# Triangular inversions of the recurrence: their first four levels on 32x32 tiles of TensorE's array in place of 64x64

## The reference

```python
lmat = jnp.where(strict, jnp.einsum("nbhcd,nbhsd->nbhcs", k_beta, kc) * decay, 0.0)
eye = jnp.eye(C, dtype=q.dtype)
rhs = jnp.concatenate([v_beta, k_beta * jnp.exp(gc)[..., None]], axis=-1)
sol = lax.linalg.triangular_solve(eye + lmat, rhs, left_side=True, lower=True, unit_diagonal=True)
```

## Time and profile before

| | us |
|---|---|
| median of 3 runs | 3714.71 |
| lowest, highest run | 3710.28, 3719.96 |
| the profiled execution, its own time | 3723.04 |
| span of the profiled instructions | 3721.2 |
| TensorE busy in the span | 3501.6 |
| VectorE busy in the span | 2381.4 |
| ScalarE busy in the span | 1693.0 |

### The profile page before, as it was taken

One profiled execution on the slowest core, in us unless ns is written; L12 is line 12 of the kernel. 1 busy time (PEld: TensorE's weight loads), 2 busy tenths in 40 slices (PEclk: granted clock), 3 DMA queues, 4 the chain that ended last, 5 costly groups with the idle time before them and its releaser, 6 DMA issues. The chain is left out here.

```text
span 3721.2 us, 74594 instructions
## 1 busy us (share of the span) xinstructions
PE 3501.6 (94%) x28666; PEld 2970.6 (80%) x28666; DVE 2381.4 (64%) x4144; ACT 1693.0 (45%) x2572; POOL 109.8 (3%) x159
## 2 busy tenths in 40 slices
PE   9999998997999999999899998888788899999998
PEld 8998887787888888888788965766676788888887
DVE  5758885665688888656643553676665766666555
ACT  5546773323455555444312443444443455555333
POOL 0000000000000000000000000221110000000000
PEclk9999999898999999999999998999997999999999
DMA  5547665444445555555322464000002455555553
GB/s 199 180 143 277 256 254 187 147 159 158 169 158 180 180 181 182 194 193 182 128 90 102 149 226 168 6 7 8 6 6 83 157 187 186 190 180 181 185 186 135
DMA packets 83114, 572.03 MB, mean 154 GB/s; under 512 B 9585, under 2 KB 11889, under 8 KB 18129
## 3 DMA queue, kind: packets, MB, share of 16 engines
q1 hardware_dynamic: 81216, 560.60, 42.5%
q0 software_dynamic: 1680, 8.36, 0.6%
HBM read 566.82 MB, written 2.10 MB: 153 GB/s over the span
## 5 line engine op out<-in xcount | busy, mean ns | idle before, releaser
L252 DVE TENSOR_TENSOR w_lo<-raw,w_hi 128x1024 fp32r<-128x1024 f32 x880 | 1037.2, 1199 | 270.7 <-ACT w_hi L245 261.4
L245 ACT ACTIVATE w_hi<-raw 128x1024 fp32r<-128x1024 f32 (+1 forms) x877 | 894.1, 1038 | 640.9 <-PE po L287 308.1
L286 PE MATMUL po<-hh,w_hi 128*128 128x512 f32 x2816 | 1000.2, 400 | 21.2 <-DVE hh L391 9.2
L287 PE MATMUL po<-hh,w_lo 128*128 128x256 f32 x2816 | 789.8, 280 | 0.0
L286 PEld LDWEIGHTS po<-hh,w_hi 128*128 128x128 f32 x2816 | 530.3, 188 | 164.3 <-issue 18.7
L287 PEld LDWEIGHTS po<-hh,w_lo 128*128 128x128 f32 x2816 | 533.1, 189 | 0.0
L286 PE MATMUL po<-ff,w_hi 128*128 128x512 f32 x1408 | 494.7, 396 | 7.9 <-DVE ff L1831 7.9
L287 PE MATMUL po<-ff,w_lo 128*128 128x256 f32 x1408 | 395.1, 281 | 0.0
L286 PEld LDWEIGHTS po<-ff,w_hi 128*128 128x128 f32 x1408 | 265.6, 189 | 69.8 <-issue 8.5
L287 PEld LDWEIGHTS po<-ff,w_lo 128*128 128x128 f32 x1408 | 267.4, 190 | 0.0
L266 PE MATMUL po<-hh,w_lo 128*128 128x256 f32 x928 | 266.0, 287 | 0.6 <-DVE w_lo L252 0.6
(11 more groups left out here) (577 smaller groups left out, 6416.7 us busy)
## 6 DMA issues: line engine op xcount, KB each, us to landing
raw<-ffn_up SPq DMA_DIRECT2D x176, 1024.0 KB, 4.8
raw<-w_in SPq DMA_DIRECT2D x112, 1024.0 KB, 4.9
raw<-ada SPq DMA_DIRECT2D x86, 1024.0 KB, 6.0
raw<-ffn_down SPq DMA_DIRECT2D x64, 1024.0 KB, 5.0
raw<-w_out SPq DMA_DIRECT2D x32, 1024.0 KB, 4.8
raw<-ffn_down SPq DMA_DIRECT2D x32, 768.0 KB, 4.2
raw<-glu SPq DMA_DIRECT2D x16, 1024.0 KB, 6.6
ada_third<-ada SPq DMA_DIRECT2D x10, 1024.0 KB, 6.5
```

What stands on the lines that cost most here:

```text
L245: act.activation(w_hi[:, k % 4, 0:width], raw[:, k // 2 % ring, (k % 2) * PW:(k % 2) * PW + width], ACT.Copy).then_inc(hi_ready, 1)
L252: dve.tensor_tensor(w_lo[:, k % 4, 0:width], raw[:, k // 2 % ring, (k % 2) * PW:(k % 2) * PW + width], w_hi[:, k % 4, 0:width].bitcast(F32 ...
L286: pe.matmul(halves(bank), hi, pair[:, :, t, :], start=first and n == 0, stop=False)
L287: mm = pe.matmul(po[bank][:, 0:T], lo, pair[:, 0, t, :], start=False, stop=last and n == len(tiles) - 1)
```

## The change

A new helper `quads_pe` issues a group of levels 1 to 4 as matmuls of 32x32 by 32x32. Partition group g (32 rows) uses the tile at row group g and column group g of the array, so four tiles on the array's diagonal. In the mask product each tile computes its own diagonal block of the 64x64 result (`own`: its columns start at 0 or 32); in the sum product it computes the 32 packed columns once. The order is block m, direction e, tile g. A group now has 32 matmuls, which will be 64 matmuls and 64 weight loads in a trace. The parts of the result outside the diagonal blocks aren't written any more; VectorE still reads all 64 columns after the mask product and multiplies them by a mask that is zero there. Level 5 uses `blocks_pe` as before. Nothing changes on VectorE, ScalarE or in the waits.

```diff
--- before.py
+++ after.py
@@ -1115,17 +1115,39 @@
             for e in range(2):
                 mm[e].then_inc(sets[e][0], 1)
 
+        def quads_pe(pe, sets, outs, lhs, rhs, own):
+
+            settle(pe)
+            for m in range(4):
+                mm = []
+                for e in range(2):
+                    for g in range(4):
+                        r, h = slice(32 * g, 32 * g + 32), g % 2 * 32
+                        c = h if own else 0
+                        last = pe.matmul(outs[e][r, m * C + c:m * C + c + 32], lhs[e][r, m, h:h + 32],
+                                         rhs[e][r, m, c:c + 32], start=True, stop=True)
+                    mm.append(last)
+            for e in range(2):
+                mm[e].then_inc(sets[e][0], 1)
+
         def inv_mask_pe(pe, n, sets, l):
             for by_pe, by_dve, (i_a, i_t, i_tt, i_p), b, want in sets:
                 pe.wait_ge(by_dve, n * 17 + (3 * l if l == 1 else 3 * l - 1))
-            blocks_pe(pe, n, sets, 2 * l - 1, [s[3][0] for s in sets], [s[2][0] for s in sets], [s[2][1] for s in sets])
+            outs, lhs, rhs = [s[3][0] for s in sets], [s[2][0] for s in sets], [s[2][1] for s in sets]
+            if l < 5:
+                quads_pe(pe, sets, outs, lhs, rhs, True)
+            else:
+                blocks_pe(pe, n, sets, 2 * l - 1, outs, lhs, rhs)
 
         def inv_sum_pe(pe, n, sets, l):
             for by_pe, by_dve, (i_a, i_t, i_tt, i_p), b, want in sets:
                 pe.wait_ge(by_dve, n * 17 + (3 * l + 1))
             lhs = [i_p if l == 5 and want == "tt" else i_tt for _, _, (i_a, i_t, i_tt, i_p), b, want in sets]
             rhs = [i_tt if l == 5 and want == "tt" else i_p[:, :, 0:C // 2] for _, _, (i_a, i_t, i_tt, i_p), b, want in sets]
-            blocks_pe(pe, n, sets, 2 * l, [s[3][1] for s in sets], lhs, rhs)
+            if l < 5:
+                quads_pe(pe, sets, [s[3][1] for s in sets], lhs, rhs, False)
+            else:
+                blocks_pe(pe, n, sets, 2 * l, [s[3][1] for s in sets], lhs, rhs)
 
         def inv_first_dve(dve, n, sets):
             for by_pe, by_dve, (i_a, i_t, i_tt, i_p), b, want in sets:
```

## The result

The changed kernel takes 3765.32 us (median of 4 runs, 3761.88 to 3770.2) against 3712.93 us before: the ratio is 1.0135, with a 95% interval of 1.0115 to 1.0154. It is slower by 52 us, outside the range of the prediction.

What follows compares the result with a forecast made beforehand. The recurrence, chiefly the inversion's products on TensorE, was taken to bound the kernel. Array gain -13.5 us plus late instructions +16 us gave +2.5 us, forecast 3717 us against the median 3714.71, range 3690 to 3755.

Steps and rivals of the forecast that it cites:

- What bounds the kernel: Only the 495 us recurrence decides; the inversion's products (line 1114) hold 19.8% of its chain of waits, 98 us.
- Array time: In groups of levels 1 to 4, the array needs 0.51 us instead of 0.93, a gain of 0.42.
- The pace of the instructions: In the new groups, matmuls start between 0.008 and 0.0145 us apart, so a group takes 0.51 to 0.93 us.
- waiting groups: Inversion groups that begin after a pause, 64 of 128 changed; forecast to stay at 0.93 us, together +1.3 us.
- queued groups: Inversion groups standing behind other matmuls, 64 of 128 changed; forecast at 0.51 us, together -21.8 us of TensorE time.
- Changes of tile size: Beside the new groups, each switch costs 0.09 us; 0.11 charged per queued group, 0.05 per waiting group.
- 0.66 us of the end: Weight of each microsecond in the inversion groups: the chain counts 98 of 149 us, turning -20.5 into -13.5 us.
- rival 4: Recurrence: shorter bursts idle TensorE, half the 128 groups run at the lower clock; 3777 us, chance 0.04.
- Delivery of the instructions: Recurrence: doubled instructions arrive late in 119 packets, 28 more stalls at 0.87 us each; +16 us.
- Rival 2: Recurrence: TensorE starves, two packets in three stall, 71 more stalls; +27 us, 3742 us, chance 0.21.
- Rival 3: New groups: tiles don't run side by side when writing one bank; +17 to +104 us, chance 0.08 including the floor on starts.
- the floor on starts: New groups: matmuls start no closer than 0.025 us, a group takes 1.6 us; +66 us, 3781 us, chance 0.03.

Runs made afterwards that it cites:

- e5: The changed kernel with 32 matmuls of 128 columns in each group of levels 1 to 4, most products using another block's matrix; ratio 1.0000 to the kernel before.
- e2: The changed kernel with half the weight loads, each matmul over two blocks' columns (64), blocks 2 and 3 using another block's matrix; ratio 1.0016 to the kernel before.
- e3: The changed kernel with 64 columns in each matmul of levels 1 to 4, same instructions and tiles; 3761.6 us, ratio 1.0132 to the kernel before.
- e4: The kernel before with sum products of levels 1 to 4 reading 32 columns once instead of 64, on 64x64 tiles; 3739.5 us, ratio 1.0056.
- e1: The kernel before, on 64x64 tiles, with each product of levels 1 to 4 issued as two halves of 32 columns; 3919 us, ratio 1.0531.

## Why the prediction was wrong, point by point

**What bounds the kernel** held: only the recurrence changed its length.

**Array time** was nearly right, 0.51 us forecast and 0.55 to 0.56 measured, and so was the end of the last matmul (0.19 us). **The pace of the instructions** was wrong for waiting groups. I took 0.93 us, since line 1985 showed one matmul per 0.014; they run at 0.55 like the queued ones, one per 0.009. The 0.014 was the four tiles' own pace, the other reading that I had named. By the sum this alone would have added 64 x 0.42 x 0.66 = 18 us of gain. The split into 64 waiting and 64 queued groups decided nothing then. It was misread besides, since pauses of weight loads and of matmuls were added and halved: before, 107 of the 160 groups begin after a pause of the weight loads and 48 after one of the matmuls. **Changes of tile size** came out at about 0.15 us from start to start, as costed, and e5 shows them covered by its groups' slightly shorter time (0.81).

**The step that failed** is the price of that array time: "a microsecond saved or lost in them is therefore worth 0.66 us of the end". It took the clock as given: the sum has no term for it, and only rival 4, at 0.04, let it fall. e2 puts a number on it. There the groups save 0.49 us each at full clock, 63 us in all or 41 by that weight, and the measured gain is none (1.0016), while the time at the lower level grew from 76 to 217 us. That the lighter groups brought the clock down, and not the pauses, is shown by e3 (43 pauses, 0.91) against e2 (7 pauses, 0.80), and by e4, where only the columns differ. The price of the clock, as an estimate, comes from e2 and e4. e2: 41 us for 141 more at the lower level, 0.29 each, if the weight of 0.66 holds. e4: 11 us (recurrence) to 21 us (medians) for 68, 0.16 to 0.31 each. The change has 218 us more there, so some 35 to 68 us. Rival 4's 62 us lie in that by luck, for its reason doesn't hold: it had TensorE idle more, and 483 of 588 us busy is the share of before (443 of 542).

**Delivery of the instructions** was the right mechanism, sized too small. 118 packets came, 119 were forecast (for the somewhat shorter stretch of the earlier trace rows). 28 more pauses were forecast at 0.87 us; 35 came with 34.6 us, 0.99 each. For the weight, e3 and e5 are the pair to compare: the same clock, 40 pauses and 39 us of them between the two (e5 has 5.2 us), and groups 0.07 us longer, worth 9 us at most. The profiled recurrences differ by 571 - 537 = 34 us, which leaves 25, or 0.64 of the pauses. The ratios differ by 0.0132, 49 us (their intervals allow some 12 either way), which leaves 40, their full length. The weight is thus between my 0.66 and 1, and the term, +16 us, should have been +22 to +35. The chain of waits speaks for the upper end: it runs through 42 of the 43.6 us of the pauses, and through all 9.0 us before. Rival 2 (3742 us, chance 0.21) was nearer than the forecast, but it still credited a gain with nothing set against it.

**Rival 3** (no tiles side by side) and the floor on starts are refuted. Four row groups wrote one bank together at 8 matmuls per tile in 0.44 us (e2), and one start per 0.009 us across tiles leaves no room for a floor of 0.025 across tiles. On both points the measurement differs from the pages of the Trainium skill that the prediction named. On one tile a matmul starts every 0.034 us (16 in 0.55), so whether a floor of 0.025 holds there the runs don't say.

**The corrected sum** for the recurrence: the array saves 128 x 0.37 x 0.66 = 31 us by the old weight; late instructions take 22 to 35; the clock takes 35 to 68. Together +26 to +72 us, around the 46 of the recurrence and the 52 of the medians. (The changes of tile size, 7 us by the prediction's terms, are left out of this.) The 31 are what the sum gives at a fixed clock, and the clock takes back that much or more. How the loss divides between clock and delivery within these bounds the runs don't say.

What stays open is what short groups would be worth at a clock that held. No kernel here had both.

## What to carry to other kernels

Before splitting small matmuls further, count records, not only columns: compare the time in which 256 of them will be used up with the times after which a trace already shows unexplained "issue" pauses, and charge these at two thirds to all of their length; the chain here speaks for all. Where TensorE's work is mostly short matmuls between waits, array time that is saved may come back as time at the lower clock: read the granted clock beside the length of the groups. Cost a matmul on its tile by the larger of its moving columns and its weight load's columns (e1, e4).

## What the runs showed of the hardware that was not expected

- The granted clock of the recurrence fell with nothing changed but the columns that matmuls of the same pace streamed: 0.93 before, 0.87 with 64 groups at 32 columns in place of 64 (e4). In the profiled execution of e1, where TensorE was busy for 740 of 800 us but with short matmuls behind weight loads, it was 0.66.
- A pause of 0.3 to 2.6 us can stand at every 256th record of TensorE, one packet of 16 KB, and ends 1.2 to 1.6 us after a packet. After the change 20 of 22 blocks that were used up in under 3 us had one, 17 of 33 of 3 to 4 us and none of 35 of over 5 us. Where the loop jumps back a pause of 2.0 to 2.6 us stands in every kernel. The others stay away when the same instructions are used more slowly (e1: 118 packets in 800 us, 3 pauses, 2 of them the loop's).
- On four 32x32 tiles matmuls of 32 columns start every 0.009 us, each with its weight load, and four row groups write one bank side by side (e2: 8 matmuls of 64 columns per tile in 0.44 us).
